# First attention: values one step later, and the order of products on TensorE turned round in every odd step

## The reference, cut to what matters

```
q = (rms_norm(q_lat, q_norm) @ w_q_up)   -> 8 heads of 64 + 32
kv = (rms_norm(kv_lat, kv_norm) @ w_kv_up) -> 8 heads of 64 (keys) + 64 (values)
...
scores = einsum('bqhd,bkhd->bhqk', qn_i, k_nope) + einsum('bqhr,bkr->bhqk', qr_i, k_rot)
p = softmax(scores)            # block of 128 queries, scale 96 ** -0.5
o = einsum('bhqk,bkhd->bqhd', p, v)
...
y = (gate_a * y_a + gate_b * (o @ w_mla_out)) @ w_out
```

## Time and profile before

| | |
|---|---|
| median of 3 runs | 1789.47 us (1789.26 to 1789.98) |
| the profiled execution | 1787.86 us |
| its span, first to last instruction | 1786.1 us |
| mean granted TensorE clock | 0.997 |
| PE busy | 1763.6 us, 99% |
| POOL, DVE, ACT busy | 1181.0 (66%), 974.3 (55%), 382.4 us (21%) |
| first attention, first score to first gate product | 526.70 to 591.57 us |
| what the chain that ended last spends in its products | L1149 2%, L1170 1%, L1158 1% of the span |

### The profile page before, as it was taken

How to read it: one execution, slowest core, us unless ns; L and a number is a source line. 1 busy time by engine, 2 the same in 40 slices (tenths; PEclk the granted TensorE clock), 3 DMA queues, 4 the chain that set the end, 5 groups by cost and what they waited for, 6 DMA issues and landing times.

```text
span 1786.1 us, 24918 instructions
## 1 busy us (share of the span) xinstructions
PE 1763.6 (99%) x8821; PEld 1394.4 (78%) x8821; DVE 974.3 (55%) x1664; ACT 382.4 (21%) x827; POOL 1181.0 (66%) x1182
## 2 busy tenths in 40 slices
PE   8999999999999999999999999999999999999998
PEld 6888888887876788888888888878446778888887
DVE  4855345544655105565514556799874887007613
ACT  3111000012246211211100001455884110000001
POOL 4676767675665477677677768755754677668862
PEclk9999999999999999999999999999999999999999
DMA  9655465542330132455435543513000322333221
GB/s 355 215 189 176 141 206 186 161 153 66 100 99 25 36 107 94 142 171 188 125 110 191 188 127 94 127 50 95 25 25 1 95 71 96 114 96 93 95 94 48
DMA packets 245549, 212.93 MB, mean 119 GB/s; under 512 B 45986, under 2 KB 240991, under 8 KB 245471
## 3 DMA queue, kind: packets, MB, share of 16 engines
q1 hardware_dynamic: 229440, 211.18, 37.0%
q10 hardware_dynamic: 16030, 0.72, 0.5%
HBM read 209.72 MB, written 2.10 MB: 119 GB/s over the span
## 4 chain that ended last, share of the span: by engine, by line
PE 70%; POOL 13%; issue 9%; DVE 5%; DMA 1%; ACT 1%; ACTq 0%; POOLq 0%; DVEq 0%
PE ps L768 19%; PE ps L770 18%; PE ps L769 18%; POOL w_lo L697 8%; POOL w_hi L692 2%; PE ps L1378 2%; POOL w_hi L691 2%; PE ps L1389 2%; PE ps L1149 2%; PE ps L1409 2%; DMA raw<-in_ffn_w_down 1%; PE ps L1170 1%; PE ps L1158 1%; PE ps L809 1%; DVE tt L2260 0%
## 5 line engine op out<-in xcount | busy, mean ns | idle before, releaser
L697 POOL TENSOR_TENSOR w_lo<-raw,w_hi 128x512 fp32r<-128x512 f32 (+4 forms) x576 | 736.3, 1307 | 11.8
L768 PE MATMUL ps<-h_hi,w_hi 128*128 128x512 f32 x1192 | 467.8, 392 | 1.8 <-DVE h_lo L2552 1.4
L770 PE MATMUL ps<-h_hi,w_lo 128*128 128x512 f32 x1192 | 464.8, 390 | 0.0
L769 PE MATMUL ps<-h_lo,w_hi 128*128 128x512 f32 x1192 | 464.6, 390 | 0.0
L689 POOL TENSOR_TENSOR w_hi<-raw,ones 128x8 fp32r<-128x8 f32 x144 | 33.3, 232 | 449.5 <-PE ps L770 385.3
L768 PEld LDWEIGHTS ps<-h_hi,w_hi 128*128 128x128 f32 x1192 | 223.9, 188 | 54.4 <-issue 5.9
L770 PEld LDWEIGHTS ps<-h_hi,w_lo 128*128 128x128 f32 x1192 | 223.9, 188 | 47.3
L769 PEld LDWEIGHTS ps<-h_lo,w_hi 128*128 128x128 f32 x1192 | 224.0, 188 | 46.2
L768 PE MATMUL ps<-g_hi,w_hi 128*128 128x512 f32 x608 | 237.7, 391 | 0.1
L770 PE MATMUL ps<-g_hi,w_lo 128*128 128x512 f32 x608 | 236.6, 389 | 0.0
L769 PE MATMUL ps<-g_lo,w_hi 128*128 128x512 f32 x608 | 236.6, 389 | 0.0
(11 more groups left out here) (408 smaller groups left out, 2405.6 us busy)
## 6 DMA issues: line engine op xcount, KB each, us to landing
ada<-in_ada_w SPq DMA_DIRECT2D x31, 1024.0 KB, 7.0
ada<-in_w_ada SPq DMA_DIRECT2D x24, 1024.0 KB, 7.2
raw<-in_ffn_w_gate SPq DMA_DIRECT2D x22, 1024.0 KB, 5.3
raw<-in_ffn_w_up SPq DMA_DIRECT2D x22, 1024.0 KB, 5.2
raw<-in_w_in SPq DMA_DIRECT2D x16, 1024.0 KB, 5.1
raw<-in_w_up SPq DMA_DIRECT2D x16, 1024.0 KB, 5.3
raw<-in_w_down SPq DMA_DIRECT2D x16, 1024.0 KB, 4.8
raw<-in_ffn_w_down SPq DMA_DIRECT2D x16, 768.0 KB, 4.8
```

The source lines that it names most:

```text
L697: last = pool.tensor_tensor(lo[:, c], src[:, c], hi[:, c].bitcast(F32), ALU.subtract)
L768: pe.matmul(o, wh, xh, start=start, stop=False)
L769: pe.matmul(o, wh, xl, start=False, stop=False)
L770: return pe.matmul(o, wl, xh, start=False, stop=stop)
```

## The change

In even steps PE's order stays (scores, transposes, values). In odd steps it is values, transposes, scores. `LAG_V1` goes from 3 to 4: step s now makes the values of step s-4. A third pair of buffers for the transposed tiles, `rb_pair`, lies over `rb` and `sq_sum`, which are free during the attention; so a copy waits for values of six tiles before instead of four. PE's two waits for the queries' evacuation stand in steps 2 and 4 instead of 2 and 3. `LAG_V1` also stands in the loops of ACT and DVE, where it moves the high and low parts of the output by one step (to steps 8, 12, 16, 20) and adds a last, empty round. The order of exponentials, copies, maxima and inverses is not touched.

```diff
+    rb_at = used[0]
     rb = place("rb", [P, T])
     sq_sum = place("sq_sum", [P, T])
...
     MLA_STEPS = 2 * MLA_HEADS
-    LAG_T1, LAG_V1 = 2, 3
+    LAG_T1, LAG_V1 = 2, 4
+    rb_pair = place("rb_pair", [P, 2, T], at=rb_at)
...
     def turned1(t):
 
-        return (sq, tt)[t // 2 % 2][:, t % 2]
+        return (sq, tt, rb_pair)[t // 2 % 3][:, t % 2]
...
         for s in range(2, MLA_STEPS + LAG_V1):
-            if s in (2, 3):
-                pe.wait_ge(q_ev, s + 1)
+            if s in (2, 4):
+                pe.wait_ge(q_ev, s // 2 + 2)
             if s == 4 + LAG_V1:
                 pe.wait_ge(rp_out, 3)
-            if s < MLA_STEPS:
+            if s % 2 and s >= LAG_V1:
+                values(s - LAG_V1)
+            if s % 2 == 0 and s < MLA_STEPS:
                 scores(s)
             if LAG_T1 <= s < MLA_STEPS + LAG_T1:
                 transposes(s - LAG_T1)
-            if s >= LAG_V1:
+            if s % 2 and s < MLA_STEPS:
+                scores(s)
+            if s % 2 == 0 and s >= LAG_V1:
                 values(s - LAG_V1)
...
         def turn(t):
             act.wait_ge(at_tr, t + 1)
-            if t >= 4:
-                act.wait_ge(at_pv, t // 2 - 1)
+            if t >= 6:
+                act.wait_ge(at_pv, t // 2 - 2)
```

## The result

The changed kernel takes 1796.99 us (median of 6 runs, 1794.62 to 1799.0), the one before, on the same chip, 1789.56 us (6 runs, 1787.98 to 1789.98). The ratio is 1.004, 95% interval 1.003 to 1.005: slower, by 7.4 us at the medians. Its profiled execution took 1796.21 us with a span of 1794.4 (before 1787.86 and 1786.1), and its mean granted clock is 0.995 (before 0.997).

What follows compares the result with a forecast made beforehand. TensorE (PE), busy 99% of the span, was taken to bound the kernel. Terms -2.5 + 3.9 + 1.7 + 0.4 + 1.4 = +4.9 us gave 1794.4 us on the median's scale, range 1791.2 to 1797.4.

Steps and rivals of the forecast that it cites:

- the forecast's own case: Whole kernel: the waits outweigh the saved switches, giving 1793.1 to 1796 us; chance 65%.
- rival 3: End of first attention: PE's rests drop the clock to 0.50 for 3.4 us, adding 1.7 us: 1796.1; chance 12%.
- signs of being wrong: Pairs of 7.3 us, even-step transposes running through in 0.88, or a difference at the gates that isn't the whole's.
- The switches, -2.5: PE in the first attention: fewer changes between scores (S), transposes (T) and values (V), 4.7 us down to 2.2.
- The steady wait, 6 x 0.65: Second tile of even-step transposes (steps 2, 4 to 12) waits 0.65 us for ACT's copy: 3.9 us lost.
- The start, +1.7: Step 1's transposes, now right behind step 0's, wait for copies still behind exponentials: 1.98 us lost, net 1.7.
- T(3), +0.4: Step 3's transposes wait for POOL's tiles: 0.4 us lost, with 0 and 0.8 as ends.
- The end, +1.4: Step 14's transposes wait for step 13's copies, 2.37 us lost; earlier waits at steps 14 and 15 go: net 1.4.
- The third pair costs nothing and buys nothing here: Third pair of transposed-tile buffers: no effect, as the copies' only idle time was waiting for a transpose, never values.
- V one step later finds its copies done: Values (V) on PE, made one step later: their copies are already finished, so no wait is added.
- Rival 1, the switches alone: First attention: copies come in time, so only saved switches count, 2.5 us, giving 1787.0 us; chance 7%.

Runs made afterwards that it cites:

- Run 1: Changed kernel, with ACT doing both copies of transposed tiles ahead of the two exponentials in odd steps: 1790.46 us, ratio 1.0004 to the kernel before.
- run 6: Changed kernel, with idle products filling PE's rests in the transposes of steps 1 and 14, ahead of all their waits: 1794.94 us, ratio 1.0029 to the kernel before.
- Run 10: Changed kernel, with two pairs of buffers for the transposed tiles instead of three: 1799.94 us, ratio 1.0065 to the kernel before.
- run 9: Changed kernel, with values three steps later instead of four and two pairs of buffers, so the turned order alone: 1811.22 us, ratio 1.0124 to the kernel before.
- run 4: Changed kernel, with ACT's copies ahead of both exponentials in every step and DVE's previous-step inverse ahead of the maxima: 1787.81 us, ratio 0.9988 to the kernel before.
- run 8: Changed kernel with copies ahead of exponentials and inverses ahead of maxima, PE's order turned only from step 6: 1786.57 us, ratio 0.9979 to the kernel before.
- run 2: Kernel before, with values one step later and the third pair of buffers, PE's order not turned: 1788.35 us, ratio 0.9994.
- run 3: Changed kernel, with idle products in the two rests of step 14's transposes, the first fill behind the wait for POOL's tile: 1796.18 us, ratio 1.0035 to the kernel before.
- run 7: Changed kernel with start and end rests filled, plus two idle products in each steady rest: 1795.44 us, ratio 1.0032 to the kernel before.

## Why the prediction was right, and where it was not

It said slower, by 4.9 us; the medians say 7.4. The sign, the place and the releaser were right, and 1796.99 lies within the range, near its upper end. It lies outside the forecast's own case, 1793.1 to 1796: what happened is the forecast's waits and the fall of rival 3 together. One of its own signs of being wrong came up in part: the profile shows 6.86 us more at the gates and 8.3 in the whole. What is over lies at the later fall of the clock, whose length varies between executions of one kernel.

- **The switches, -2.5.** T to S is free again, and V to T costs 1.02 - 0.88 = 0.14 us (taken: 0.15). Right. The Trainium skill's rule on draining, which the prediction cited (TensorEngine Tiling (Array Packing), Key Properties), gives the right sign for this term; taken alone it gives the wrong one for the kernel.
- **The steady wait, 6 x 0.65.** T's tiles start at 558.65 and 559.74: 1.09 less 0.44, 0.65 us, and a pair takes 7.91 (said: 7.9). T(2) alone lost a little more, 0.72. Run 1 shows the cause: the same PE order without the rest when the copies don't stand behind exponentials.
- **The start, +1.7.** T(1)'s tiles at 537.11 and 538.26, S(3) at 538.73, where T(0), begun at 534.75, would let T(1) run through by 536.75: 1.98 us lost, as said.
- **T(3), +0.4.** It starts 0.3 late, by POOL, and takes 1.16 instead of 0.88: near 0.6, within the ends of 0 and 0.8 but more than taken.
- **The end, +1.4.** T(14) at 590.25 and 591.41, 1.65 and 0.72 us of rest: 2.37, as said; T(15) without a rest, as said. 2.37 less the 1.01 of before is 1.36.
- **The sum** of these, about 5.1, beside the 5.25 of the stretch without the slow clock, and 5.2 in run 6, which has none there. The working was sound to a few tenths.
- **What failed is the clock.** The forecast kept it out and gave it to rival 3, with 12%: "the rests are shorter and broken, and rests of 0.4 before left it at 1.00". The two rests of the end are not like those of 0.4. In both profiles of the changed kernel PE stood 1.65 us, worked 0.44, stood 0.72 more (not twice 1.2, as the prediction split the same sum), and then ran at 0.50 for about 3.4 us; in run 1 the rests of the start, 1.2 and 0.7, were followed by the same. The price worked out for it, 1.7 us, was right (3.43 instead of 1.90 for two V, and the last products of T: 1.6). The term was left out of the sum, and its chance was too low: the nearest row of a rest and a fall, 2.6 us long, stood nearer to the new end than the rests of 0.4 did.
- **Forecast with that term:** 1796.1 (rival 3), 0.9 from the median. That remainder is not settled; the falls elsewhere vary by 1.7 us from one execution to the next. That a forecast without the fall still has its range around the result owes something to the width which rival 3 gave it.
- **"The third pair costs nothing and buys nothing here"** was wrong in its second half. It was argued from the copies of before, which never waited for values; but in the turned order the values of a step stand later against its copies. Run 10: without it 3.7 us more. What ought to have been read is the new order, not the old idle time.
- **"V one step later finds its copies done"**: right, and it is what the step is for (run 9 against run 10, which has two pairs as well: 11 us).
- **Rival 1, the switches alone,** asked for copies that end by 2.01 us behind their scores. They didn't in the change. In run 4 and run 8 the steady copies came in time: -3.15 and -3.4 us in the stretch, of which 1.0 came without the turned order (run 2).

## What to carry to other kernels

Turning the order of work on the engine that bounds a kernel turns the time at which its results are wanted; engines that serve it in order, here ACT with exponential, copy, exponential, copy, must be turned with it, or the saved switches are paid back as waits. Put first, on each serving engine, what is ready and waited for (a copy out of a shared bank; an inverse too, though here its share was not measured by itself), and behind it what waits for the newest product. And where a change brings new rests to a TensorE that was full, look for the nearest rows of a rest and of the clock behind it, and cost the clock too; here rests of 0.65 us were free of it and 1.65 with 0.72 were not.

## What the runs showed of the hardware

- The granted clock fell to 0.50 behind rests of 1.65 and 0.72 us with 0.44 us of work between them, in all four profiles that have them (the changed kernel twice, runs 9 and 10). In the changed kernel the fall lasted some 3.4 us and cost about 1.6. Behind rests of 1.2 and 0.7 us at the start it fell in one profile (run 1) and not in four others (the changed kernel twice, runs 3 and 10). Idle products in the rests of the end kept it at 1.00 (runs 3, 6 and 7). The Trainium skill (TensorE: Matmul & The Clock Gate, A second HAM failure mode: psum-queue depth-cycling) tells of a kernel whose short rests between groups of products made the clock go up and down and cost throughput. By that the steady rests would be suspect too. The trace doesn't show it: the pairs with rests of 0.65 us ran at 1.00, and filling them (run 7) changed nothing. Behind the longer ones of the end the clock did fall.
- It also falls while PE is busy: ahead of the second attention, at 8.00 us busy of 8.00, it showed 0.79, 0.57 and 0.59 over 8 us in three profiles (before, changed, run 8). In all twelve profiles this fall begins inside or right behind a group of 64 products of 32 columns (before it runs from 1231.1 to 1234.9 us, and the clock is lower from about 1235). Whether that group sets it off, and why the fall is 3.4 us long in two profiles and 6.8 in ten, stays open. It is a part of the 4 to 5 us over which the executions of one kernel spread (before, beside the experiments: 1787.6 to 1792.4).
